# u laid out transposed by the host, with one load, one copy and one subtraction per block

## The reference, cut to what matters

```python
q = (xb @ peer_wq).reshape(PEER_BLOCK, PEER_HEADS, 2, PEER_HALF)
s = jnp.einsum('thpd,pkd->thpk', q, peer_subkeys).astype(jnp.float32)
sv, si = lax.top_k(s, PEER_TOPK)
...
fv, fi = lax.top_k(cand, PEER_TOPK)
eidx = jnp.take_along_axis(cidx, fi, axis=-1)
gate = jax.nn.softmax(fv, axis=-1).astype(xb.dtype)
act = jax.nn.gelu(jnp.einsum('thkd,td->thk', peer_u[eidx], xb))
return jnp.einsum('thk,thkd->td', gate * act, peer_v[eidx])
```

## Time and profile before

| | |
|---|---|
| median of 3 runs | 4282.88 us (4282.53 to 4288.63) |
| the profiled execution | 4279.69 us, its span 4278.0 us |
| TensorE's clock granted, mean | 0.977 of full speed |
| busy: PE | 4077.9 us, 95% |
| busy: DVE | 2592.4 us, 61% |
| busy: ACT | 1390.0 us, 32% |
| busy: POOL | 714.2 us, 17% |
| transfers | 943.10 MB, 220 GB/s over the span |

### The profile page before, as it was taken

One profiled execution on the slowest core, in us unless ns is written; L12 is line 12 of the kernel. 1 busy time (PEld: TensorE's weight loads), 2 busy tenths in 40 slices (PEclk: granted clock), 3 DMA queues, 4 the chain that ended last, 5 costly groups with the idle time before them and its releaser, 6 DMA issues.

```text
span 4278.0 us, 69824 instructions
## 1 busy us (share of the span) xinstructions
PE 4077.9 (95%) x26191; PEld 3935.2 (92%) x26191; DVE 2592.4 (61%) x4092; ACT 1390.0 (32%) x1876; POOL 714.2 (17%) x514
## 2 busy tenths in 40 slices
PE   8998979979889979999999999999999999999996
PEld 6788969979849979999999999999999999999996
DVE  3324232351453266666477556666679899898896
ACT  3433221132442132222355422222233333333333
POOL 0000020020000030044100001111123333344430
PEclk9989989989999999999999999999999999999998
DMA  6542222213542212233344599999999999999994
GB/s 224 196 117 55 82 59 79 78 50 118 197 138 79 78 54 77 97 117 121 113 171 169 195 315 355 354 350 355 355 339 403 397 411 409 394 400 396 402 384 135
DMA packets 495289, 943.10 MB, mean 220 GB/s; under 512 B 126372, under 2 KB 375904, under 8 KB 443032
## 3 DMA queue, kind: packets, MB, share of 16 engines
q1 hardware_dynamic: 443552, 567.36, 39.8%
q0 software_dynamic: 51616, 374.19, 21.8%
HBM read 866.63 MB, written 73.56 MB: 220 GB/s over the span
## 4 chain that ended last, share of the span: by engine, by line
PE 91%; DVE 4%; DMA 2%; ACT 2%; DVEq 1%; issue 1%; POOL 0%; SPq 0%; ACTq 0%
PE pl L1127 25%; PE pp L197 24%; PE pp L1186 12%; PE pt L1186 6%; PE pl L1186 6%; PE pp L1095 5%; PE pt L1104 2%; PE pp L792 2%; PE pt L792 1%; PE pl L792 1%; PE pp L859 1%; DMA kv<-in_cache_mem_k 1%; DMA raw<-in_w_mk 1%; PE pl L821 1%; PE pt L823 1%; PE pl L1046 1%
## 5 line engine op out<-in xcount | busy, mean ns | idle before, releaser
L1127 PE MATMUL pl<-h_hi,ut_hi 128*128 128x384 f32 x2048 | 734.7, 359 | 0.6 <-ACT ijt L1465 0.6
L1127 PE MATMUL pl<-h_hi,ut_lo 128*128 128x384 f32 x2048 | 692.1, 338 | 0.0
L1127 PE MATMUL pl<-h_lo,ut_hi 128*128 128x384 f32 x2048 | 691.3, 338 | 0.0
L1838 DVE TENSOR_TENSOR ut_lo<-pp,ut_hi 128x512 fp32r<-128x512 f32 x508 | 350.2, 690 | 483.3 <-ACT ut_hi L1418 479.1
L1418 ACT ACTIVATE ut_hi<-pp 128x512 fp32r<-128x512 f32 x508 | 304.1, 599 | 820.6 <-PE pp L1095 763.4
L212 DVE TENSOR_TENSOR w_lo<-raw,w_hi 128x2048 fp32r<-128x2048 f32 x120 | 274.8, 2291 | 424.0 <-ACT w_hi L207 424.0
L1490 ACT ACTIVATE v_hi<-v_raw 128x1024 fp32r<-128x1024 f32 x256 | 271.9, 1062 | 682.6 <-PE pl L1186 438.3
L1940 DVE TENSOR_TENSOR v_lo<-v_raw,v_hi 128x1024 fp32r<-128x1024 f32 x256 | 313.2, 1223 | 123.3 <-ACT v_hi L1490 122.6
L1127 PEld LDWEIGHTS pl<-h_lo,ut_hi 128*128 128x128 f32 x2048 | 387.1, 189 | 0.0
L1127 PEld LDWEIGHTS pl<-h_hi,ut_hi 128*128 128x128 f32 x2048 | 386.2, 189 | 0.8 <-ACT ijt L1465 0.8
L1127 PEld LDWEIGHTS pl<-h_hi,ut_lo 128*128 128x128 f32 x2048 | 384.7, 188 | 0.0
(11 more groups left out here) (387 smaller groups left out, 8257.7 us busy)
## 6 DMA issues: line engine op xcount, KB each, us to landing
u_raw<-in_peer_u SPq DMA_DIRECT2D x256, 512.0 KB
v_raw<-in_peer_v SPq DMA_DIRECT2D x256, 512.0 KB
p_f<-p_scr SPq DMA_DIRECT2D x256, 192.0 KB
raw<-in_w_in SPq DMA_DIRECT2D x24, 1024.0 KB, 5.6
g_scr<-gs POOLq DMA_DIRECT2D x6, 4096.0 KB, 13.6
raw<-in_w_mk SPq DMA_DIRECT2D x16, 1024.0 KB, 4.9
raw<-in_w_mv SPq DMA_DIRECT2D x16, 1024.0 KB, 4.8
raw<-in_w_out SPq DMA_DIRECT2D x16, 1024.0 KB, 5.9
```

The lines of the kernel that those rows point to most:

```text
L1127: last = mm(pl[:, d, 0:N], w[:, d, k, :], x[:, k, S:S + N], start=(k == 0 and w is ut_hi and x is h_hi), stop=(k == KC - 1 and w is ut_lo))
L1838: tt(ut_lo[:, d, 4 * g:4 * g + 4, :], src.rearrange("p (c i) -> p c i", c=4), ut_hi[:, d, 4 * g:4 * g + 4, :].bitcast(F32), ALU.subtract). ...
```

## The change

The host lays out u once more as peer_ut: block b is a 128 x 2048 array with the contraction on the partitions: 16 pieces of 128 x 128 side by side, each turned, in the order in which `turn_rows` and `rows_hi` left them in ut_hi. `turn_rows`, `t_done` and the transposes go. A block of u is now one load of 1 MB, which waits for `t_lo` (the subtraction of the block before in the same slot), one copy by ACT (128x2048), from SBUF and no longer from PSUM, which waits for the load and for the end of the column two before, and one subtraction by DVE. Column b waits once for `t_lo`, at its start. The order of the work around it moves too:
- PICK 32 to 28, AHEAD 60 to 56, STEP_COL 62 to 58. `next_rows` puts in one subtraction where it put in two, counting halves.
- one_hot is three operations over four tokens (128x512) in place of eight of 128x128.
- The gates are loaded for four columns at a time (`gate_fours`, buffers g4 and a4) in pieces of 1 KB rather than 256 bytes, and once for b and once for b - 56.
- SP's order in the steady stretch: the block of u, the two stores, s, and every fourth column the gates. `upto` is 5/4 of a step per column, plus 3/4 from column 112 on.
- The columns' PSUM banks move from pl to pp; the last query panel's evacuation moves behind column 0's start, with one half list of DVE.

```diff
-PICK = 32
-AHEAD = 60
-STEP_COL = 62
+PICK = 28
+AHEAD = 56
+STEP_COL = 58
 STEP_M = 246
-GELU_S = 43
+GELU_S = 46
...
+        a4 = [at("a4_0", Y_HI + 57344, [P, 2 * ND, 4, HALF]), at("a4_1", TMP + 12800, [P, 2 * ND, 4, HALF])]
-        u_in = [[sem(f"u_in{s}{h}") for h in range(2)] for s in range(2)]
-        t_done, t_hi, t_lo = sem("t_done"), sem("t_hi"), sem("t_lo")
+        u_in = [sem(f"u_in{s}") for s in range(2)]
+        t_hi, t_lo = sem("t_hi"), sem("t_lo")
...
-            def u_load(i, d, h, free=None):
+            gv = g_scr.rearrange("h p (q i) t -> q p h i t", i=4)
                 if free is not None:
-                    sp.wait_ge(t_done, free)
-                sp.dma_start(u_raw[:, d, h * HD:(h + 1) * HD], uv[i * 2 + d][:, h * HD:(h + 1) * HD])\
+                    sp.wait_ge(t_lo, free)
+                sp.dma_start(u_raw[:, d, :], uv[i * 2 + d]).then_inc(u_in[d], 16)
+            def next_u(i, d):
+                u_load(i + 1, d, i * 2 + (d + 1))
...
+            def p_store(b):
+                sp.wait_ge(gm_done, gated_count(b))
+                sp.dma_start(p_scr[b], fg[:, b % 2, :]).then_inc(f_stored[b % 2], 16)
+            def gate_fours(k, both=True):
+                for dst, q in ((g4, k + AHEAD // 4),) + (((a4, k),) if both else ()):
+                    sp.dma_start(dst[k % 2][:, :, :, :], gv[q]).then_inc(g4_in[k % 2], 16)
...
+            def ahead_steady(j, d, b=None):
+                s = d % 2
+                sp.wait_ge(t_lo, j * 8 + (d + 1))
+                sp.dma_start(u_raw[:, s, :], uv[j * 8 + (d + 2)]).then_inc(u_in[s], 16)
                 if b == AHEAD:
+                    for x in range(2):
+                        sp.wait_ge(g_stored[x], 16 * ND)
+                    for k in range(2):
+                        gate_fours(k)
...
+                    sp.wait_ge(gm_done, j * 16 + (2 * (d - AHEAD) - 2))
+                    sp.dma_start(p_scr[j * 8 + (d - AHEAD - 2)], sa[:, s, :]).then_inc(pa_stored[s], 16)
+                    sp.wait_ge(gm_done, j * 16 + (2 * (d - AHEAD) - 3))
+                    sp.dma_start(p_scr[j * 8 + (d - 2)], fg[:, s, :]).then_inc(f_stored[s], 16)
+                if b is None or b >= AHEAD + 2:
+                    sp.wait_ge(pa_stored[s], j * 64 + (16 * (d // 2 - AHEAD // 2)))
+                else:
+                    sp.wait_ge(f_stored[s], 16 * AHEAD // 2)
+                sp.dma_start(sa[:, s, :], s_scr[j * 8 + (d - AHEAD)]).then_inc(s_in[s], 16)
+                if d % 4 == 1 and (b is None or b > AHEAD + 1):
+                    x = (d // 4 + 1) % 2
+                    sp.dma_start(g4[x][:, :, :, :], gv[j * 2 + (d // 4 + 1)]).then_inc(g4_in[x], 16)
+                    if b is None or b < 2 * AHEAD - 4:
+                        sp.dma_start(a4[x][:, :, :, :], gv[j * 2 + (d // 4 + 1 - AHEAD // 4)]).then_inc(g4_in[x], 16)
...
             for b in range(2 * AHEAD, NK):
+                s = b % 2
+                if b + 2 < NK:
+                    next_u(b // 2, s)
+                if b < 2 * AHEAD + 2:
+                    sp.wait_ge(gm_done, 2 * (b - AHEAD) - 2)
+                    sp.dma_start(p_scr[b - AHEAD - 2], sa[:, s, :]).then_inc(pa_stored[s], 16)
+                p_store(b - 2)
+                if b % 4 == 1 and b + 4 < NK:
+                    gate_fours((b - AHEAD) // 4 + 1, False)
...
-            def turn_rows(i, d, g, dst, first=False):
-                if g % 2 == 0:
-                    pe.wait_ge(u_in[d][g // 2], i * 16 + 16)
-                if first:
-                    if g >= 2:
-                        pe.wait_ge(t_lo, g - 1)
-                else:
-                    pe.wait_ge(t_lo, i * 8 + (4 * d + g - 3))
-                for c in range(4):
-                    last = turn(dst[:, c * P:(c + 1) * P], u_raw[:, d, (4 * g + c) * P:(4 * g + c + 1) * P], ident[:, :])
-                last.then_inc(t_done, 1)
...
-            def column(i, d, gate=None, more=True):
-                if not (isinstance(i, int) and i == 0):
+            def column(i, d, gate=None):
+                start = isinstance(i, int) and i == 0
+                if start:
+                    pe.wait_ge(evacuated, NPANEL - 1)
+                else:
                     pe.wait_ge(ge_done, i * 2 + (d - 1))
                 for k in range(KC):
-                    if k % 4 == 0:
-                        pe.wait_ge(t_lo, i * 8 + (4 * d + k // 4 + 1))
+                    if k == 0:
+                        pe.wait_ge(t_lo, i * 2 + (d + 1))
                     for w, x in ((ut_hi, h_hi), (ut_hi, h_lo), (ut_lo, h_hi)):
-                        last = mm(pl[:, d, 0:N], w[:, d, k, :], x[:, k, S:S + N],
+                        last = mm(pp[0][:, d, 0:N], w[:, d, k, :], x[:, k, S:S + N],
                                   start=(k == 0 and w is ut_hi and x is h_hi), stop=(k == KC - 1 and w is ut_lo))
                     if k == KC - 1:
                         last.then_inc(u_done, 1)
-                    if k % 4 == 1:
-                        if more:
-                            turn_rows(i + d, 1 - d, k // 4, turn_bank(k // 4))
-                        if gate is not None:
-                            gate_matrix(group(gate, k // 4)[0], k // 4 % 2)
+                    if start and d == 0 and k == 7:
+                        select_scores(NPANEL - 1, 1)
+                    if gate is not None and k % 4 == 1:
+                        gate_matrix(group(gate, k // 4)[0], k // 4 % 2)
                 if isinstance(i, int) and 1 <= 2 * i + d <= 8:
...
-            panel(wq_use, split=False)(num(NPANEL - 1), 15)
+            def rows_hi(i, d, used=None):
+                act.wait_ge(u_in[d], i * 16 + 16)
                 if used is not None:
                     act.wait_ge(u_done, used)
-                f(ut_hi[:, d, 4 * g:4 * g + 4, :], src.rearrange("p (c i) -> p c i", c=4), ACT.Copy).then_inc(t_hi, 1)
+                f(ut_hi[:, d, :, :], u_raw[:, d, :].rearrange("p (c i) -> p c i", c=KC), ACT.Copy).then_inc(t_hi, 1)
-            def column(i, d, gate=None, more=True):
+                f(fg[:, d, :], pp[0][:, d, 0:N], ACT.Gelu_apprx_tanh).then_inc(ge_done, 1)
+            def column(i, d, gate=None):
                 first = isinstance(i, int) and i == 0 and d == 0
                 for g in range(4):
-                    if more:
-                        rows_hi(i + d, 1 - d, g, turn_bank(g), None if first or g else i * 2 + d)
+                    if g == 0:
+                        if first:
+                            act.wait_ge(panel_done, NPANEL)
+                        rows_hi(i + d, 1 - d, None if first else i * 2 + d)
+                    if first and g == 1:
+                        scores_out(15)
...
-            act.wait_ge(panel_done, NPANEL)
             f(ident_r[:, :], ident[:, :], ACT.Copy).then_inc(xr_out, 1)
-            for g in range(4):
-                rows_hi(0, 0, g, pt[g % 2][:, :])
-                if g == 1:
-                    scores_out(15)
+            rows_hi(0, 0)
+            panel(wq_use, split=False)(num(NPANEL - 1), 15)
...
+            def rows_lo(i, d):
+            turned, asked = [0], [0]
...
-            def rows_lo(i, d, g, src):
-                dve.wait_ge(t_hi, i * 8 + (4 * d + g + 1))
-                tt(ut_lo[:, d, 4 * g:4 * g + 4, :], src.rearrange("p (c i) -> p c i", c=4),
-                   ut_hi[:, d, 4 * g:4 * g + 4, :].bitcast(F32), ALU.subtract).then_inc(t_lo, 1)
-            turned = [0]
-            def next_rows(count=2):
-                for _ in range(count):
-                    n = turned[0]
-                    if n < 4 * (PICK + 1):
-                        rows_lo(n // 8, n // 4 % 2, n % 4, pt[n % 2][:, :] if n < 4 else turn_bank(n % 4))
-                        turned[0] += 1
-            next_rows(4)
+            next_rows(2)
+            half_list(2 * PH - 3)
+            next_rows(2)
             for c in (2 * PH - 2, 2 * PH - 1):
                 half_list(c, next_rows)
             for h in range(PH):
                 pick(h)
-            while turned[0] < 4 * (PICK - 1):
+            while turned[0] < PICK - 1:
                 next_rows(1)
...
             dve.drain()
-            while turned[0] < 4 * (PICK + 1):
-                next_rows(1)
+            next_rows(2 * PICK, PICK + 1)
...
-            def one_hot(n, s, t0):
-                if not (isinstance(n, int) and n < 2):
+            def one_hot(n):
+                s = n % 2
+                if n >= 2:
                     dve.wait_ge(g_done, n - 1)
-                for x in range(4):
-                    ts(oh[:, s, 0, x, :], iota_k[:, :], ijt[:, 1, bass.ds(t0 + x, 1)], None, ALU.is_equal)
-                    last = ts(oh[:, s, 1, x, :], iota_k[:, :], ijt[:, 0, bass.ds(t0 + x, 1)],
-                              ijt[:, 2, bass.ds(t0 + x, 1)], ALU.is_equal, ALU.mult)
-                last.then_inc(oh_ready, 1)
-            def gate_column(i, d, gate):
+                def of(x):
```

(48 more changed lines are left out.)

129 lines of the change are left out of this document (50 added, 79 removed).

## The result

| | before | changed |
|---|---|---|
| median | 4284.93 us (4 runs) | 4228.11 us (4 runs, 4218.00 to 4235.33) |
| ratio of the changed kernel to the one before | | 0.9865 (95% interval 0.9842 to 0.9888) |
| span of the profiled execution | 4278.0 us | 4233.6 us |
| time by stage, from GELU to GELU, of the profiled execution: | | |
| start to the GELU of column 0 | 1772.3 | 1768.5 |

(The columns before 58 have no number of before, since its gate stretch lies elsewhere.) The change is faster by 1.35%, where 4.8% was forecast. In columns 58 to 111 the kernel without transposes is slower than the one with them. The page of the changed kernel (against the earlier trace rows) shows the place: in slices 24 to 28 PE falls to 8 and 7 tenths, its clock to 8 in three of them, and the transfers to 286 to 306 GB/s, where before had 315 to 355.

A forecast was written before the change was run, and what follows sets the result against it. The prediction took PE as the bound: 4278.0 - 218.6 - 1.7 (transposes) + 2 + 10.6 (picking) - 1.3 (gw_ready wait) + 5 (SP's wait) = 4074.0 us of span, written as 4078 for the median; range 4054 to 4130.

The forecast's parts named there:

- 2 + 10.6: Picking: 2 us lost to GpSimd excluding VectorE's subtractions, plus one 10.6 us PE stall before column 27.
- 23 x 12.2: Gate stretch: a column takes 12.2 us on PE without transposes, VectorE's at most 10.7 us hidden behind it.
- 54 x 8.46 + 5: Steady stretch: plain columns of 8.46 us each, plus 5 us for SP's wait, bounds 0 and 76.
- The transposes: All columns but the last: removing them saves 1.72 us each on PE, 220.3 us with those before column 0.
- 5.9 + 3.8 = 9.7 us: Steady stretch: u's load plus the longest earlier wait for the s product's store, which would exceed a column's 8.46 us.
- 395 GB/s against 404: Steady stretch: 3.34 MB per 8.46 us column needs 395 GB/s; 404, seen in the value stage, would hide it.
- 1.25 gathered blocks per column: Steady stretch: gathered rows per column, 1.049 MB each, counted within 3.34 MB of transfers per column.
- The rival "slower": Steady stretch and on: u's loads behind the store, SP in single file, 11.3 us per column, 4283 and more; chance 0.03.
- The first rival: From column 56 on: DMA becomes the bound at 380 to 356 GB/s, total 4092 to 4149; chance 0.26.
- The exclusion: Picking: VectorE's subtraction with two SBUF inputs and a GpSimd instruction block each other wholly; 2 us lost in all.
- the rival of every head: Picking: GpSimd's 5.7 us product delays the first subtraction in every head, 35 us in place of 2, 4111; chance 0.13.
- The value stage: Final stage: same steps left and same matmuls as before, so a change of 0.

The follow-up runs named there:

- e11: Four-buffer s kernel (e9) with stores and s issued before u, gates loaded in thirds and the double gather step moved two columns; 4103.07 us, ratio 0.9561.
- e6: Changed kernel with no gather steps before column 84 and two per column from there, both GELUs of the gathered part later; 4202.98 us (one run).
- e9: Changed kernel with four buffers for s in place of two and six gather buffers in place of seven; 4124.20 us, ratio 0.9615.
- e5: Changed kernel with the one column in four that has two gather steps moved by two columns; 4188.15 us, ratio 0.9774.
- e7: Changed kernel without GpSimd's product and three sums per head in picking, so the output differs; 4205.26 us (one run).
- e1: Changed kernel with SyncE issuing the stores and loading s before the block of u in columns 58 to 111; 4180.32 us, ratio 0.9752.
- e12: Changed kernel with both stores issued from ScalarE's queue, gates in thirds and the double gather step moved two columns; 4161.52 us, ratio 0.9701.

## Why the prediction was wrong

The sum forecast 4074.0 us of span; 4233.6 came, 159.6 more. By stretch, with the prediction's own terms:

| stretch | forecast | measured | off |
|---|---|---|---|
| to the GELU of column 0 | 1772.3 - 1.7 = 1770.6 | 1768.5 | -2.1 |
| columns 1 to 27: 27 x 8.46, 5.7 of sparse rows as before, 2 + 10.6 | 246.7 | 258.0 | +11.3 |
| columns 28 to 51: 23 x 12.2, and 20.2 - 1.7 - 1.3 | 297.8 | 293.3 | -4.5 |
| columns 52 to 57 | 50.8 | 50.6 | -0.2 |
| columns 58 to 111: 54 x 8.46 + 5 | 461.8 | 602.2 | +140.4 |
| columns 112 to 127 | 135.4 | 135.1 | -0.3 |
| from there to the end | 1112.8 | 1125.9 | +13.1 |

They sum to 157.7. The forecasts by stretch add up to 4075.9 and not to 4074.0, since one sum counts up columns and the other takes transposes off; that is the other 1.9.

**The transposes.** Right: 8.43 us where 8.46 was forecast, 12.00 where 12.2 was, and all of it on PE. In the plain columns copy, subtraction and load are hidden, as forecast.

**The step that failed: the steady stretch.** The prediction named the wait ("SP now stands in line for the landing of the s product's store behind a whole block of u"), worked out 5.9 + 3.8 = 9.7 us against 8.46, and then booked 5 us for all columns. The wait was 8.1 us on the mean of the 54 columns, and 16.4 at the worst. Two things were missing. First, SP's cycle is this wait plus the 3.0 us in which it issues the rest, 8.1 + 3.0 = 11.15, and nothing behind the wait goes out meanwhile: when the store has landed the queue holds little more, and the DMA engines, at a share of 1.02 before, have 0.83. The prediction asked whether the bytes fit (395 GB/s against 404; they do, e11 carries 386) and not whether they can be asked for in time. Second, it reckoned with 1.25 gathered blocks per column as a mean. Two of them come in one column of four, the one with the gates, and there the landing takes 15. e6 shows that the wait is harmless without the gathers (8.4 us), e9 that without the wait the gathers and the rest cost 0.7 us a column and not 2.7 (9.18), e5 that the coincidence is worth 0.97 us a column, e11 that with all of it mended the forecast pace is there, 8.51. A second wait has no term in the prediction at all: GELU's for the landing of fg's store, 424.5 us in 47 times. It remains in e9 (224.9 us, 9.18 a column) and has nearly gone in e11 (75.6 us, 8.51).

The stretch took 145.4 us more than 54 x 8.46. 116.9 of them are PE's waits; the rest is PE itself, which was busy 485.3 us for what takes e11 457.0, 28.3 more. Behind the twelve long stalls stand 145 matmuls that come 0.32 us apart and not 0.176, the clock being at 0.50 of full speed there: 21 of the 28.3. The prediction had no term for that either.

The rival "slower" had this very mechanism with too low a price: it decides at 11.3 us per column in all 72 columns, and 11.15 was measured in 54 of them. The last 16 columns, with no s to load and so without the wait, ran at 8.44 at 399 GB/s. Had they and columns 56 and 57 run at 11.15 too, the time would have been some 49 us more, 4277, still just below the 4283 from which that rival counts. The first rival (DMA as the bound, 4092 to 4149) would have had the engines busy; they were not. The Trainium skill, "DMA: Bandwidth & Descriptors" (section "Specifications"), gives some 358 GB/s as HBM's limit for a core. The trace does not agree, with one core running: e11 has 386 GB/s over 459 us.

**Picking.** The mechanism was right, its frequency mis-sized. The exclusion cost 2 us in the sum and some 11.5 in the trace (columns 7, 10, 13, 16 and 22 take 2.8, 1.6, 3.9, 1.4 and 1.8 more): a subtraction met the product itself, as in the rival of every head, in some heads and not in all. e7, without the product and the sums, has none of it. Which heads are hit differs between runs that are alike up to there (column 16 takes 9.8 us here, 8.4 in e1 and e11), while the 27 columns together stay at 257.6 to 258.0 in every run with this picking but e12 (254.3). The Trainium skill, "SBUF — State Buffer" (section "SBUF: two separate sides"), lets whichever starts first block the other wholly; the trace agrees in both directions: 7.02 us for a subtraction of 2.29 alone, and 4.26 for POOL's candidates of 2.38, asked for at 1975.10 behind this subtraction:

```profile
1974.85 2.28 DVE L1822 TENSOR_TENSOR ut_lo<-u_raw,ut_hi 128x2048 fp32r<-128x2048 f32 x1
```

 Before column 27 10.6 us were forecast and 11.25 came, 1.8 with POOL's product left out where 2 was said; what the prediction had not is the half clock behind it.

**The value stage.** 13.1 us more, forecast 0. PE waits 8.6 us once at the turn of the two passes for DVE's r, and 4.3 us for p_lo at the start, against 1.6 and 1.8 before, 9.5 of the 13.1 together. Why DVE comes later to the same steps was not tried. It did not go away in any run (1121 to 1133 us from the last column to the end).
